# A recursion on (I+L)X in place of X, in the recurrent chunks of a two-block network

## The reference, cut to what matters

```python
def rwkv_scan(state0, terms, reverse, with_output):
    ...
    def step(S, inp):
        w_t, k_t, v_t, a_t, b_t = inp[-5:]
        sa = jnp.einsum('bhvk,bhk->bhv', S, a_t)
        S = S * w_t[:, :, None, :] + sa[..., None] * b_t[:, :, None, :] + v_t[..., None] * k_t[:, :, None, :]
        y_t = jnp.einsum('bhvk,bhk->bhv', S, inp[0]) if with_output else None
        return S, y_t
    S, ys = lax.scan(step, state0, xs, reverse=reverse)
```

## Time and profile before

| | |
|---|---|
| median of 3 runs | 2548.6 us (2547.74 to 2555.16) |
| span of the profiled execution, first to last instruction | 2544.3 us |
| between the two | 4.3 us |
| PE busy, mean granted clock | 94%, 0.985 of full |
| the two recurrent stretches | 471.7 to 630 us and 1076.2 to 1229 us |
| matmuls of L1793, L1805, L1810 (the recursion) | 2304, 1536 and 1920 |

### The profile page before, as it was taken

How to read it: one execution, slowest core, us unless ns; L and a number is a source line. 1 busy time by engine, 2 the same in 40 slices (tenths; PEclk the granted TensorE clock), 3 DMA queues, 4 the chain that set the end, 5 groups by cost and what they waited for, 6 DMA issues and landing times.

```text
span 2544.3 us, 48745 instructions
## 1 busy us (share of the span) xinstructions
PE 2389.8 (94%) x20392; PEld 1886.3 (74%) x20392; DVE 1333.1 (52%) x2131; ACT 1000.0 (39%) x1675; POOL 167.8 (7%) x217
## 2 busy tenths in 40 slices
PE   6999999888989999888899998999999999999999
PEld 5777777777857776777666666788887667788887
DVE  5347644566364653555467773555424665555422
ACT  3225453444343444344445554322223454322222
POOL 0000000444000000144000000000000010000000
PEclk9999999999999999999999999999999999999999
DMA  8721111000102111100131212233333222233332
GB/s 289 248 69 34 35 44 52 17 5 12 58 25 79 44 40 54 47 4 5 57 94 58 59 50 67 75 98 99 97 94 116 58 66 75 83 99 92 99 94 79
DMA packets 300551, 182.65 MB, mean 72 GB/s; under 512 B 5290, under 2 KB 284476, under 8 KB 300236
## 3 DMA queue, kind: packets, MB, share of 16 engines
q1 hardware_dynamic: 286940, 150.50, 20.2%
q10 hardware_dynamic: 12480, 25.17, 2.8%
q0 software_dynamic: 944, 4.27, 0.5%
HBM read 177.80 MB, written 2.12 MB: 71 GB/s over the span
## 4 chain that ended last, share of the span: by engine, by line
PE 80%; DVE 9%; ACT 5%; issue 2%; DVEq 2%; ACTq 1%; DMA 0%; SPq 0%
PE PW L323 11%; PE PW L325 11%; PE PW L324 11%; PE PW L413 6%; PE PW L414 6%; PE PW L415 6%; PE PW L1267 2%; PE PW L1224 2%; PE PW L1810 2%; PE PW L1805 1%; PE PW L1793 1%; DVE wlo L245 1%; PE PW L3012 1%; PE PW L980 1%; PE PW L598 1%
## 5 line engine op out<-in xcount | busy, mean ns | idle before, releaser
L245 DVE TENSOR_TENSOR wlo<-wraw,whi 128x1024 fp32r<-128x1024 f32 (+1 forms) x272 | 328.7, 1209 | 378.5 <-ACT whi L238 357.3
L238 ACT ACTIVATE whi<-wraw 128x1024 fp32r<-128x1024 f32 (+1 forms) x272 | 283.7, 1043 | 268.1 <-PE PW L325 256.4
L413 PE MATMUL PW<-hhi,whi 128*128 128x512 f32 (+1 forms) x880 | 324.9, 369 | 11.7 <-DVEq L3221 7.0
L323 PE MATMUL PW<-hhi,whi 128*128 128x512 f32 (+1 forms) x824 | 315.6, 383 | 0.0
L324 PE MATMUL PW<-hhi,wlo 128*128 128x512 f32 (+1 forms) x824 | 315.2, 382 | 0.0
L325 PE MATMUL PW<-hlo,whi 128*128 128x512 f32 (+1 forms) x824 | 315.1, 382 | 0.0
L414 PE MATMUL PW<-hhi,wlo 128*128 128x512 f32 (+1 forms) x880 | 307.5, 349 | 0.0
L415 PE MATMUL PW<-hlo,whi 128*128 128x512 f32 (+1 forms) x880 | 307.1, 349 | 0.0
L413 PEld LDWEIGHTS PW<-hhi,whi 128*128 128x128 f32 x880 | 168.4, 191 | 57.4 <-issue 24.0
L414 PEld LDWEIGHTS PW<-hhi,wlo 128*128 128x128 f32 x880 | 168.6, 192 | 22.1 <-issue 3.4
L415 PEld LDWEIGHTS PW<-hlo,whi 128*128 128x128 f32 x880 | 168.5, 191 | 22.1
(11 more groups left out here) (478 smaller groups left out, 4420.6 us busy)
## 6 DMA issues: line engine op xcount, KB each, us to landing
wraw<-in_w_in SPq DMA_DIRECT2D x68, 512.0 KB, 3.8
mod_w<-in_mod_w ACTq DMA_DIRECT2D x12, 2048.0 KB, 10.1
wraw<-in_ffn_w_gate SPq DMA_DIRECT2D x44, 512.0 KB, 3.7
wraw<-in_ffn_w_up SPq DMA_DIRECT2D x44, 512.0 KB, 3.7
wraw<-in_ffn_w_down SPq DMA_DIRECT2D x32, 512.0 KB, 3.8
wraw<-in_attn_w_in SPq DMA_DIRECT2D x24, 512.0 KB, 3.7
wraw<-in_w_out SPq DMA_DIRECT2D x16, 512.0 KB, 3.8
wraw<-in_rg_w_in SPq DMA_DIRECT2D x16, 512.0 KB, 4.0
```

What stands on the lines that cost most here:

```text
L238: act.activation(whi[:, slot, 0:kb, :], wraw[:, slot, 0:kb, :], ACT.Copy).then_inc(S("w_hi"), 1)
L245: dve.tensor_tensor(wlo[:, slot, 0:kb, :], wraw[:, slot, 0:kb, :], whi[:, slot, 0:kb, :].bitcast(F32), ALU.subtract).then_inc(S("w_split"), 1)
L323: pe.matmul(acc, wh[:, k, :], rhi[:, k0 + k, s0:s1], start=a, stop=False)
L413: e.matmul(acc, whi[:, u % 2, k, :], rhi[:, k0 + k, s0:s1], start=k == 0, stop=False)
```

## The change

It carries U = (I+L)X and not X. A level is U' = UT, T' = mask(UT): the same product UT gives both, so that a level has its transposed form (16 products of `pe_level`, next T, masked by DVE) and its plain form (16 products, next U transposed, copied by ACT into UT). `p1` falls away. The level's two products are issued for both directions in one step, and one step of DVE (`dve_T`, 128x512) and one of ACT (`act_U`, 128x512) serve both. At the end X = (U+I)/2: `dve_inverse` adds I, and `act_xa` scales by 0.5. T and U have banks of their own (2, 3 and 4, 5), T two buffers. The backward direction's blocks cross the halves (`tp = half(pi ^ d)`), where before the odd heads' did.

The own terms stay in PSUM: `pe_chain` adds onto them (start=False), `act_own`, OWN, the step "y_own" and the wait for it go, `decayed` is one product on DVE in place of four scaled adds, `dve_y` adds all of y once.

```diff
+            def both_ways():
+                for r_ in range(4):
+                    for d, pi in ((0, 0), (0, 1), (1, 0), (1, 1)):
+                        yield d, r_, pi, 4 * d + r_, half(pi), half(pi ^ d)
...
+            def T_at(d, r_):
+                return bank(2 + d)[:, CH * r_:CH * r_ + CH]
+            def U_at(d, r_):
+                return bank(4 + d)[:, CH * r_:CH * r_ + CH]
+            def pe_turned_L(e, j):
+                wait(e, unit, 1, j, 1)
+                for d, r_, pi, dh, rp, tp in both_ways():
+                    ins = e.matmul(T_at(d, r_)[rp, :], MB[j % 2][rp, dh, 0, :], ident2[rp, :], start=True, stop=True)
                 ins.then_inc(T_made.sem, 1)
+            def pe_level(e, j, lv):
+                def operands(dh, rp, tp):
+                    if lv == 0:
+                        return Tt[0][rp, dh, :], MB[j % 2][rp, dh, 0, :], rp
+                    src, out = (rp, tp) if lv % 2 else (tp, rp)
+                    return Tt[lv % 2][src, dh, :], UT[src, dh, :], out
+                wait(e, T_out, 6, j, lv + 1)
+                if lv:
+                    wait(e, U_out, 5, j, lv)
+                if lv < 5:
+                    for d, r_, pi, dh, rp, tp in both_ways():
+                        t_, ut, out = operands(dh, rp, tp)
+                        ins = e.matmul(T_at(d, r_)[out, :], ut, t_, start=True, stop=True)
+                    ins.then_inc(T_made.sem, 1)
+                for d, r_, pi, dh, rp, tp in both_ways():
+                    t_, ut, out = operands(dh, rp, tp)
+                    ins = e.matmul(U_at(d, r_)[out, :], t_, ut, start=True, stop=True)
+                ins.then_inc(U_made.sem, 1)
...
                 wait(e, kw_out, 2, j, 2)
-                wait(e, X_out, 10, j, 10)
+                wait(e, inverse, 1, j, 1)
...
                         l_, r_ = ((G[re, g, :], ST[re, 2 * d + hp, :]), (ST[re, 2 * d + hp, :], QT[re, g, :]))[what]
-                        ins = e.matmul(own_at(d, hp, pi, re, what, j), l_, r_, start=hp + what == 0,
-                                       stop=hp == 1 and what == int(has_y(j)))
+                        ins = e.matmul(own_at(d, hp, pi, re, what, j), l_, r_, start=False, stop=False,
+                                       skip_group_check=True)
...
+            def act_U(a, j, lv):
+                wait(a, U_made, 6, j, lv + 1)
+                a.activation(UT[:].rearrange("p (d r) b -> p d r b", d=2), both_banks(2), ACT.Copy).then_inc(U_out.sem, 1)
...
-                a.activation(AW[j % 2].rearrange("p (g e) c b -> p e g c b", e=2)[:, e_, :, 1::-1, :], src, ACT.Copy) \
-                 .then_inc(xa_out.sem, 1)
+                a.activation(AW[j % 2][:, 4 * d:4 * d + 4, 1::-1, :], xa_block(d), ACT.Identity, scale=0.5).then_inc(xa_out.sem, 1)
...
+            def dve_T(v, j, lv):
+                wait(v, T_made, 6, j, lv + 1)
+                mask = levels[:, lv, :, :].unsqueeze(2).to_broadcast([P, 2, 4, CH])
+                v.tensor_tensor(Tt[lv % 2][:].rearrange("p (d r) b -> p d r b", d=2), both_banks(1), mask, ALU.mult) \
+                 .then_inc(T_out.sem, 1)
+            def dve_inverse(v, j):
+                wait(v, U_made, 6, j, 6)
+                same = ident2.unsqueeze(1).unsqueeze(1).to_broadcast([P, 2, 4, CH])
+                v.tensor_tensor(UT[:].rearrange("p (d r) b -> p d r b", d=2), both_banks(2), same, ALU.add) \
+                 .then_inc(inverse.sem, 1)
...
+                for name, j, lv in (
+                        ("turned_L", s, 0), ("xa", b, 0), ("xa_out", b, 0), ("xa_out", b, 1), ("level", s, 0),
+                        ("between", b, 0), ("kw", s, 0), ("gq", b, 0), ("kw_out", s, 0), ("QT", b, 0), ("level", s, 1),
+                        ("own", b, 0), ("own", b, 1), ("level", s, 2), ("decayed", b, 0), ("ends", a, 0), ("Lb", a, 0),
+                        ("mask_b", a, 0), ("chain", b, 0), ("state", b, 0), ("level", s, 3), ("mask_b", a, 1), ("decayed", b, 1),
+                        ("Lk", a, 0), ("chain", b, 1), ("state", b, 1), ("level", s, 4), ("mask_k", a, 0), ("mask_k", a, 1),
+                        ("unit", a, 0), ("y", b, 0), ("level", s, 5), ("ab", a, 0), ("ab_out", a, 0), ("decays", a + 1, 0),
+                        ("r_decays", a + 1, 0)):
```

More of the change, by code:

```diff
@@ L1729, in rwkv @@
             QT_out = Signal("rw_QT_out", NBATCH - first_y)
-            owned, own_out, y_own, chain, y_added = (count(n_, m_) for n_, m_ in (
-                ("owned", 1), ("own_out", 1), ("y_own", 1), ("chain", 2), ("y_added", 1)))
+            owned, chain, y_added = (count(n_, m_) for n_, m_ in (("owned", 1), ("chain", 2), ("y_added", 1)))
             state = Signal("rw_state", 2 * NBATCH - 1)
@@ L1761, in half, with quarters @@
                 return slice(64 * i, 64 * i + 64)
-            def quarters(ds=(0, 1)):
-                for d in ds:
+            def quarters():
+                for d in range(2):
                     for hp in range(2):
                         for e_, pi in ((0, 0), (1, 1), (0, 1), (1, 0)):
-                            yield d, hp, e_, pi, 4 * d + 2 * hp + e_, half(e_), half(pi), half(pi ^ e_)
+                            yield d, hp, e_, pi, 4 * d + 2 * hp + e_, half(e_), half(pi), half(pi ^ d)
@@ L1781, in pe_p1 @@
[L1781 to L1793, removed]
-                ins.then_inc(T_made.sem, 1)
@@ L1849, in pe_turned @@
                     wait(e, BK_made, 2, j, 2)
+                    for d, hp, e_, pi, dh, re, rp, tp in quarters():
+                        a = (2 * d + hp) * CH
+                        e.matmul(bank(e_)[tp, a:a + CH], AR_of(j)[re, d, hp, 0, rp], ident2[re, :], start=True, stop=True)
                 else:
                     wait(e, ab_out, 2, j, 2)
[L1852 to L1858, removed]
+                    for d, r_, pi, dh, rp, tp in both_ways():
+                        e.matmul(bank(d)[tp, r_ * CH:r_ * CH + CH], MK[j % 2][rp, dh, 0, :],
+                                 vtok[rp, T[d], r_ * CH:r_ * CH + CH], start=True, stop=True)
                 for d in range(2):
@@ L1932, in pe_last_own @@
                                 l_, r_ = ((vv, MKj[rp, dh, 1, :]), (AWj[rp, dh, 0, :], MBj[rp, dh, 1, :]))[part]
-                            ins = e.matmul(own_at(d, hp, pi, re, what, LAST, True), l_, r_, start=part + step + hp + what == 0,
+                            ins = e.matmul(own_at(d, hp, pi, re, what, LAST), l_, r_, start=part + step + hp + what == 0,
                                            stop=part + step + hp + what == 4)
@@ L1943, in pe_chain @@
                         wait(e, QT_out, 1, j - first_y, 1)
-                    else:
-                        wait(e, y_own, 1, j, 1)
+                    wait(e, owned, 1, j, 1)
                     if j:
@@ L2062, in dve_unit @@
                 v.tensor_tensor(L, L, ident2.unsqueeze(1).to_broadcast([P, 8, CH]), ALU.add).then_inc(unit.sem, 1)
[L2064 to L2081, removed]
-                v.tensor_tensor(T, src, mask, ALU.mult).then_inc(T_out.sem, 1)
+            def dve_T(v, j, lv):
[8 more added lines that the diff above has]
+                 .then_inc(inverse.sem, 1)
             def dve_QT(v, j):
@@ L2135, in slot @@
                 if s == 0:
-                    instead = {("xa_out", b, 0): "mask_k0", ("gq", b, 0): "mask_k1", ("QT", b, 0): "ab", ("own", b, 0): "ab_out",
-                               ("own_out", b, 0): "kw", ("y_own", b, 0): "kw_out"}
+                    instead = {("xa", b, 0): "mask_k0", ("xa_out", b, 0): "mask_k1", ("xa_out", b, 1): "ab", ("between", b, 0): "ab_out"}
                 elif s == LAST:
@@ new lines, in slot @@
+                for name, j, lv in (
[6 more added lines that the diff above has]
+                        ("r_decays", a + 1, 0)):
+                    if 0 <= j < NBATCH and name != "between":
+                        yield name, j, lv
@@ L2187, in act_scan @@
                 a.preload_act_table_set("natural_log_exp_and_others")
-                for name, j, lv, d in program:
-                    if name == "p23":
-                        act_X(a, j, lv, d)
+                for name, j, lv in program:
+                    if name == "level" and lv < 5:
+                        act_U(a, j, lv)
                     elif name == "xa_out":
@@ L2215, in dve_scan @@
                 v.drain()
-                for name, j, lv, d in program:
-                    if name == "p1":
-                        dve_T(v, j, lv, d)
+                for name, j, lv in program:
+                    if name == "turned_L":
+                        dve_T(v, j, 0)
+                    elif name == "level" and lv < 5:
+                        dve_T(v, j, lv + 1)
+                    elif name == "level":
+                        dve_inverse(v, j)
                     elif name == "QT":
```

130 lines of the change are left out of this document (48 added, 82 removed).

## The result

The changed kernel takes 2525.1 us in the median of 4 runs (2519.3 to 2529.7), the kernel before 2548.2: 23.1 us less, a ratio of 0.9905 (95% interval 0.9884 to 0.9927). The forecast was 2518, from 2500 to 2536. The gain came, with three quarters of its size.

A forecast was written before the change was run, and what follows sets the result against it. The PE was taken as the bound, paced by instruction supply. Twelve slots of 266.0 us against 295.7, plus 1 in the tails, save 31: span 2544.3 becomes 2513, plus 4.3 to the median gives 2518 us, range 2500 to 2536.

The forecast's parts named there:

- What bounds the slot: PE in a full slot: code arrives in packets of 128 matmuls with their weight loads, about 3.65 us each.
- Rival A: Code supply doesn't pace the thinner program, so full slots take 21.1 us: 2498 us in all; chance 0.18.
- Fewer products, and their rate: Recursion on PE: 384 products a slot instead of 480, levels 1 to 5 in four quarters; 3.5 us less per slot.
- Rival C: Levels 1 to 5 miss the four-quarter rate and add 4.3 us a slot: 2551 us in all; chance 0.05.
- The waits of the walk: PE waits added up step by step through a full slot with known durations and hand-overs: 3.4 us together.
- Pauses: PE waits for code in a full slot, three of six stretches under the packet's pace: 2.3 us.
- Rival B: Waits under-reckoned by 1 us a slot and a packet pace of 3.83 us: 2534 us in all; chance 0.22.
- the slots without y: Two slots: 18.5 us by adding up steps, 19.4 by 5.3 packets, taken as 20.3 each, 40.6 together.
- Rival D: DVE's end of slot: unit and inverse stretch beside POOL's work, full slots 27.6 us, 2568 us in all; chance 0.03.
- First slots: Each layer's first slot, steps and waits added up to 21.0 us; with code pauses 21.2 each, 42.4 for two.
- Tails: Stretch behind the last slot of each layer: y_own no longer ahead of the chain, 0.5 us less a layer.
- The sum: All twelve slots: 266.0 us against 295.7, 29.7 less, and 1 at the layers' ends: 31 us less.

The follow-up runs named there:

- the second part stood alone: Kernel before with only the own terms kept in PSUM and one DVE product for the decayed state, old recursion: 2548.1 us, ratio 0.9996 to the kernel before.
- the last slot was mended: Changed kernel with dummy products in first slots and ahead of the last xa, block 3's rounding moved behind inverse: 2514.9 us, ratio 0.9865 to the kernel before.

## Why the prediction was right, and where it was off

**What bounds the slot: right.** Instruction supply as the pace was read from pauses every 128 matmuls. Three runs bear it out from three sides: a wait taken off the PE gives nothing, work in few instructions is partly free, the same work in 128 instructions costs a packet. The end of each pause stands behind the landing of a packet. Rival A (no such pace) is thereby out for this program: after has pauses of up to 1.8 us in its full slots. The Trainium skill, "Runtime: NRT & Kernel Launch", section Instruction fetch mechanics, says that the cost of crossing into the next block of code is mostly hidden; by these runs it is not (the pauses take 2.4 us of a full slot), and the measurement decides.

**Fewer products, and their rate: right.** 777 matmuls a full slot (776 by the count) and 18.1 to 18.7 us busy in five of the six, 19.1 in the sixth (18 to 19). The timeline of after, a level 0 and a level 1:

```profile
523.63 1.13 PE L1806 MATMUL PW<-Tt,MB 64*64 64x64 f32 x32
...
527.60 0.64 PE L1806 MATMUL PW<-Tt,UT 64*64 64x64 f32 x32
528.06 0.65 PE L1810 MATMUL PW<-UT,Tt 64*64 64x64 f32 x32
```

Level 1's 64 take 1.11 us with the tail (1.0 and 0.22 in the working), level 0's, in two quarters, 2.05. Rival C is out. (Its 4.3 us counted 64 instructions for level 5, which has 32: 3.9.)

**The waits of the walk: right.** `Lk` 1.0 us a slot (1.15), level 5 0.82 (0.95), `own` behind QT 0.52 (0.7), `ab` and `xa` behind `inverse` no row at all (0.35 and 0.2). They look high because the working counts the last product's tail of 0.22 us as wait and the profile as busy; less the tail they are 0.93, 0.73 and 0.48. Pauses were 9.5 / 4 = 2.4 us a slot (2.3). Full slot 23.5 (23.4). That the mean came out so near is partly luck: the six slots spread from 22.6 to 25.35 us, and of the slots without y the working gives 18.5 and 19.4 us and then takes 20.3 without saying how. Rival B is out by the waits and by the mean of the full slots, though not by the time alone: 2525.1 lies 7 us from the forecast and 9 from B. Rival D never showed, `unit` took 0.69 us in all twelve slots.

**First slots: wrong by 3.8 us each.** The working added up products and waits at full clock, although in the earlier trace rows a first slot had a clock of 0.93 already. The term that is missing is the clock's: by an estimate from the clock column the PE ran at the lower level for 13.7 us of the slot, and before for 3.4. At full clock the untouched slot took 20.13 us and the two with dummies 20.5 to 21.1, so the walk's 21.2 was 1.1 too long and the clock's 4.9 were left out. The first slots are 7.7 of the 12.3 us by which the span missed the sum. That fewer products brought the clock down is likely but not shown: the new first slot had 0.73 in eight of ten untouched cases, 0.92 in one and 1.00 in one, and the old one had 0.93 in all four.

**Tails: wrong by about 2.7 us.** They took 7.85 and 6.82 us where 5.8 and 6.1 would have been the sum's. In layer 0 it was the clock. In the run with dummies in the first slot alone the PE waited 2.45 us for `inverse` as well, but the clock stayed up behind it:

```profile
616.37:622.06 5.69, 5.35 (x224) 1.00 0.02 6
```

5.69 us at 1.00, 7.85 at 0.68: the sum's 5.8 was right at full clock, and the wait does not bring the lower clock each time. In layer 1 it was not the clock alone. Three of the runs above had the full clock there and took 6.8 to 7.0 us, with a code pause of 1.0 to 1.2 us ahead of `gq`; the changed kernel took 6.82 at 0.79 without that pause. The working had no pause in its tails. The 0.5 us that `y_own` should have given were not there when the second part stood alone (6.34 and 6.63 us, as before). And the walk of the last slot had DVE's weight rounding ahead of the first state, but not block 3's ahead of `inverse`, which the PE waits for. The last slots themselves were 21.97 and 21.74 (21.3).

**The sum.** 7.7 + 2.7 + 1.1 for the last slots + 0.6 for the full ones are the 12 us between the 31 forecast and the 18.7 measured. The time missed by only 7 us, and that is luck: the forecast added 4.3 us, the distance from the span of one profiled execution to the median. In the kernel after, the median lies 0.5 us below the profiled span (and 1.8 us lie between the profiled execution's own time and its span), so 4.8 us of the miss were made good by a term that says nothing of the kernel. For the same reason the medians moved by 23.1 us where the two spans moved by 18.7: single executions of one kernel lie up to 8 us from their median here.

## What to carry over

Where many small products follow each other, count instructions and not only busy time: if the pauses that nothing explains come at a fixed count of instructions, the fewest instructions win, and covering a wait or relieving another engine gives nothing until the pace does. An edit that takes work off the PE in a stretch full of bare waits must be checked against the granted clock of that stretch; dummy products in those waits gave 4 us a first slot here, though the kernel as a whole gained clearly only when the last slot was mended as well. In an in-order engine's list, look at the seam between two stages for a result that somebody waits for behind work that nobody does.

## What was new of the hardware

- Code supply has a pace of its own: between pauses 128 matmuls took 3.45 to 4.03 us before, in the slots looked at packets of code began 3.28 us apart or more, and 123 matmuls more in a slot with unchanged busy time took 2.1 us more (26.7 against 24.6). The pace varies: five full slots with the same steps took 25.1 to 28.3 us.
- With 128 matmuls of 2 columns more a slot, the full slots of layer 0 had clocks of 0.83 to 0.94; with the same 128 of 64 columns three of the four had 1.00 and one 0.94.
- How deep the clock falls in a first slot differs between executions and layers, with the same code: 0.73, 0.92 or 1.00, for 25.03, 22.04 or 20.13 us. What decides it is open.
